# Low halves of all weight tiles made by VectorE, at the place in its order where GpSimd had them

## The reference

```python
h = _rmsnorm(x, norm_g[i])
u = h @ (w_in_a, w_in_b, w_in_c)[kind][j]          # mixer columns, 4 memory-query heads, gate
br = mixer_A | mixer_B | mixer_C                   # layers 0..3: A, B, C, A
mo = _mem_attend(mq, mem_k[i], mem_v[i])           # 4 heads over 256 memory tokens
y = concat([br, mo]) * silu(gate)
x = x + y @ w_out[i]
```

## Time and profile before

| | |
|---|---|
| median of 3 runs | 3066.82 us (3064.26 to 3069.39) |
| profiled execution | 3064.44 us, of which the span from first to last instruction is 3062.7 us |
| granted TensorE clock, mean over the span | 0.950 of full speed |
| PE, PEld | 2791.3 us (91%), 2613.0 us (85%) |
| DVE, ACT, POOL | 1301.4 us (42%), 1312.9 us (43%), 693.6 us (23%) |
| instructions in the span | 46628 |

### The profile page before, as it was taken

One profiled execution on the slowest core, in us unless ns is written; L12 is line 12 of the kernel. 1 busy time (PEld: TensorE's weight loads), 2 busy tenths in 40 slices (PEclk: granted clock), 3 DMA queues, 4 the chain that ended last, 5 costly groups with the idle time before them and its releaser, 6 DMA issues.

```text
span 3062.7 us, 46628 instructions
## 1 busy us (share of the span) xinstructions
PE 2791.3 (91%) x18936; PEld 2613.0 (85%) x18936; DVE 1301.4 (42%) x3217; ACT 1312.9 (43%) x2822; POOL 693.6 (23%) x389
## 2 busy tenths in 40 slices
PE   6989999989989999989988578888899989999987
PEld 4979999979989999979988567777699979999887
DVE  4045555551235665651232244544433054555542
ACT  3244454442244555542332245555533244544431
POOL 0212122205121222205120222222233212221112
PEclk9989999999999999989998789999899989999998
DMA  3111111123111111123110000000042111111121
GB/s 137 50 39 49 50 63 45 48 113 106 51 45 50 60 61 59 60 106 110 56 42 32 22 12 10 9 10 7 15 169 72 56 35 51 57 48 55 41 76 66
DMA packets 58197, 171.59 MB, mean 56 GB/s; under 512 B 6720, under 2 KB 15040, under 8 KB 57472
## 3 DMA queue, kind: packets, MB, share of 16 engines
q1 hardware_dynamic: 57984, 168.62, 16.1%
HBM read 134.67 MB, written 33.92 MB: 55 GB/s over the span
## 4 chain that ended last, share of the span: by engine, by line
PE 79%; ACT 9%; DVE 8%; issue 3%; DMA 0%; POOL 0%; SPq 0%; DVEq 0%; ACTq 0%
PE acc L1611 37%; PE acc L1687 10%; PE acc L1574 9%; PE scores L1632 8%; PE turned L1646 6%; PE scores L1528 4%; ACT prob L1098 4%; DVE prob L1354 2%; PE turned L1528 2%; PE scores L1506 1%; DVE pt_split L1383 1%; ACT pt_split L1110 1%; DVE y_sb L1410 1%; ACT prob L1101 1%; ACT w_hi L1028 1%
## 5 line engine op out<-in xcount | busy, mean ns | idle before, releaser
L1611 PE MATMUL acc<-h_split,w_hi 128*128 128x352 f32 (+2 forms) x4860 | 892.5, 330 | 45.0 <-ACT raw L982 13.2
L1611 PEld LDWEIGHTS acc<-h_split,w_hi 128*128 128x128 f32 x4860 | 791.7, 191 | 71.3 <-ACT raw L982 16.6
L1437 POOL TENSOR_TENSOR w_lo<-w_raw,w_hi 128x1024 fp32r<-128x1024 f32 (+2 forms) x154 | 332.2, 2159 | 1830.1 <-ACT w_hi L1028 1830.1
L1354 DVE CUSTOM_DVE_ANT_0 prob<-scores,bias 128x256 f32<-128x256 f32 (+9 forms) x576 | 337.7, 633 | 499.8 <-PE scores L1632 496.3
L1383 DVE TENSOR_TENSOR pt_split<-turned,pt_split 128x512 fp32r<-128x512 f32 (+4 forms) x564 | 303.3, 552 | 552.0 <-ACT pt_split L1110 551.6
L1687 PE MATMUL acc<-pt_split,v_split 128*64 128x256 f32 (+6 forms) x3486 | 501.4, 280 | 23.5 <-ACT pt_split L1110 7.4
L1611 PE MATMUL acc<-h_split,w_lo 128*128 128x352 f32 (+2 forms) x2430 | 453.6, 324 | 0.0
L1098 ACT ACTIVATE prob<-prob,stat 128x256 f32<-128x256 f32 (+9 forms) x468 | 303.7, 650 | 329.3 <-DVE stat L1354 329.2
L1687 PEld LDWEIGHTS acc<-pt_split,v_split 128*64 128x64 f32 (+2 forms) x3486 | 404.0, 161 | 41.2 <-issue 15.4
L1611 PEld LDWEIGHTS acc<-h_split,w_lo 128*128 128x128 f32 x2430 | 401.2, 189 | 0.1
L1646 PE MATMUL turned<-ident,prob 128*128 128x128 f32 (+2 forms) x1866 | 290.1, 280 | 98.4 <-DVE prob L1370 52.0
(11 more groups left out here) (124 smaller groups left out, 2796.9 us busy)
## 6 DMA issues: line engine op xcount, KB each, us to landing
w_raw<-w SPq DMA_DIRECT2D x132, 512.0 KB, 3.7
x_scr<-y_sb SPq DMA_DIRECT2D x24, 528.0 KB, 5.6
y_sb<-x_scr SPq DMA_DIRECT2D x24, 528.0 KB, 7.9
y_sb<-x_in SPq DMA_DIRECT2D x16, 528.0 KB, 10.5
mw_raw<-w SPq DMA_DIRECT2D x16, 512.0 KB, 7.4
bias<-rel_in SPq DMA_DIRECT2D x24, 320.0 KB, 4.0
raw<-kcache SPq DMA_DIRECT2D x18, 256.0 KB, 4.0
v_cache<-vcache SPq DMA_DIRECT2D x18, 256.0 KB, 4.0
```

The costliest lines, as they stand in the source:

```text
L1354: dve.tensor_tensor_reduce(out=prob[0:tile.rows, at:at + tile.width], in0=s_ps[lane][0:tile.rows, tile.at:tile.at + tile.width], in1=bias[ ...
L1437: pool.tensor_tensor(w_lo[:, n % 2, 0:wide], w_raw[:, n % 2, 0:wide], w_hi[:, n % 2, 0:wide].bitcast(F32), ALU.subtract).then_inc(wlo_made ...
L1611: ins = pe.matmul(acc[s.bank][:, 0:s.cols], w[ws][:, 128 * k:128 * k + 128], x(xs, k), start=k == 0 and y == 0, stop=k == s.k_tiles - 1 an ...
```

## The change

DVE makes `w_lo` of every tile, at the place of the `wsplit` in its own order; POOL no longer does. The arithmetic, the tiles, the semaphores and every other engine's order stay as they are. Of 156 tiles 154 change hands: 130 of 1024 columns, 12 of 384 and 12 of 256.

```diff
-            elif name == "wsplit" and item[1] < 2:
+            elif name == "wsplit":
                 n = item[1]
+                wide = 128 * plan.weights[n][2]
                 dve.wait_ge(*whi_made.upto(n))
-                dve.tensor_tensor(w_lo[:, n, :], w_raw[:, n, :], w_hi[:, n, :].bitcast(F32),
+                dve.tensor_tensor(w_lo[:, n % 2, 0:wide], w_raw[:, n % 2, 0:wide], w_hi[:, n % 2, 0:wide].bitcast(F32),
                                   ALU.subtract).then_inc(wlo_made.mark(n), 1)
...
-            if name == "wsplit" and item[1] >= 2:
-                n = item[1]
-                wide = 128 * plan.weights[n][2]
-                pool.wait_ge(*whi_made.upto(n))
-                pool.tensor_tensor(w_lo[:, n % 2, 0:wide], w_raw[:, n % 2, 0:wide],
-                                   w_hi[:, n % 2, 0:wide].bitcast(F32), ALU.subtract).then_inc(wlo_made.mark(n), 1)
-            elif name == "phase":
+            if name == "phase":
```

## The result

| | before | after |
|---|---|---|
| median | 3066.82 us (5 runs, 3063.80 to 3069.39) | 3080.22 us (5 runs, 3077.91 to 3085.82) |
| ratio, 95% interval | | 1.0053 [1.0039, 1.0066] |
| span of the profiled execution | 3062.7 us | 3076.1 us |
| granted clock of the profiled execution | 0.950 | 0.947 |

What follows compares the result with a forecast made beforehand. PE was taken as the bound, busy 91% of the span with 79% of the last chain. Terms 5.0 + 1.3 + 2.6 + 0.9 − 1.4 = +8.4 us on 3064.4 give 3072.8, forecast 3075 against the median, range 3064 to 3092.

Steps and rivals of the forecast that it cites:

- That nothing is gained by an earlier `w_lo`: No engine waited for POOL's tile and two buffers give slack, so having it 1.1 us earlier gains nothing.
- DVE isn't the bound: DVE gains about 168 us of work, from 1301 to about 1470 us, 48% of the span; not a bound.
- The places of A (+5.0): Ten decoded-unit starts in A: DVE 0.66 us late, PE's slack 0.24 at most; about 0.50 us lost each, +5.0.
- the starts (+1.3): First scores of each layer's memory jobs queue behind `w_lo`, so ACT's exponential starts 0.33 us late: 4 × 0.33 = +1.3.
- decoded units (+2.6) of the memory jobs: PE already waits 1.29 us for DVE's multiply; the new order puts it 0.66 us later: 4 × 0.66 = +2.6.
- Key parts (+0.9): First key part of the second memory job: exponentials move 0.66 us against 0.36 slack; 0.3 us in three layers, +0.9.
- B (−1.4): The norm's multiply no longer waits beside POOL's `w_lo`; PE regains 0.28 us in each of five jobs, −1.4.
- The output projections, costed at nothing in the sum: The 30 low halves standing in the output projections add no term to the sum; left to the rivals.
- The rival: Output projections: POOL's sum and `mw_lo` hold DVE's scalings; PE 1.12 us late per tile, +13.4, about 3088; chance 0.18.
- The clock, named as a rival on the faster side only: PE's mean granted clock rises from 0.950 to about 0.955, bringing back 14.5 us, about 3058; chance 0.08.
- the forecast's own range: Whole kernel: 3070.5 to 3080 us, with the small terms somewhat larger or smaller; chance 0.50.
- the band that it gave to contention: 3080 to 3094 us, if scalings in the output projections wait for POOL, once or twice in part; chance 0.18.

Runs made afterwards that it cites:

- Experiment 4: Changed kernel, but POOL keeps 33 low halves (21 at A's ten places and in memory jobs, 12 ahead of the scalings): 3065.43 us against 3065.13 before, ratio 1.0004.
- experiment 8: Changed kernel with output-projection scalings first and 24 low halves behind DVE's next scores: 3067.71 us against 3064.66 for the kernel before, ratio 1.0011.
- Experiment 5: Changed kernel, but DVE makes the low half twice in a row at the ten places of A: 3094.13 us, ratio 1.0099 to the kernel before.
- experiment 2: Changed kernel, but POOL makes the 30 low halves of the output projections: 3079.08 us, ratio 1.0047 to the kernel before.
- experiment 3: Changed kernel, but DVE does the output projections' two scalings ahead of the weight's low half: 3078.34 us, ratio 1.0050 to the kernel before.
- experiment 6: Changed kernel, but POOL's sum of squares in the four tiles adds 32 columns instead of 1056: 3076.97 us, ratio 1.0041 to the kernel before.
- experiment 7: Changed kernel, but POOL makes the memory weight's low half behind those of the two scaled slices: 3077.48 us, ratio 1.0042 to the kernel before.
- experiment 10: Kernel before, with only the ten low halves at the places of A moved to DVE: 3076.15 us, ratio 1.0037.
- experiment 1: Kernel before, with only the 30 low halves of the output projections moved to DVE: 3072.14 us against 3065.13, ratio 1.0027.
- experiment 9: Kernel before, with only the 14 low halves in the memory jobs moved to DVE: 3077.40 us against 3063.21, ratio 1.0046.
- experiment 11: Kernel before, with only the 16 low halves in B's mixer jobs moved to DVE: 3067.02 us against 3063.21, ratio 1.0007.
- experiment 12: Kernel before, with only the 62 low halves of the gate stages and C moved to DVE: 3067.70 us against 3063.21, ratio 1.0009.

## Why the prediction was right, and where not

- **That nothing is gained by an earlier `w_lo`, and that DVE isn't the bound:** right. Experiment 4 carries 121 of the moved instructions at no measurable cost, experiment 8 all 154 at 3 us.
- **The places of A (+5.0), the starts (+1.3) and decoded units (+2.6) of the memory jobs:** right in mechanism and size, 5.0, 1.5 and 2.7 in the trace. One name was wrong: the low half that arrives late at the places of A isn't the decoded unit's; it is the fourth unit's second chunk, which stands on DVE behind the decoded unit's scales. Experiment 5 shows that DVE's queue sets these ends, and experiment 8 that the order ahead of the low half is what costs. Read in the same way against the kernel before, the traces of experiments 2, 3, 5, 6, 7 and 10 have 5.0 to 5.1 at this step of the ten places, and those of 1, 4, 8, 9, 11 and 12, where no weight's low half stands ahead of it, 0.0 to 0.1.
- **Key parts (+0.9):** mis-sized, 0.2 where it could be read.
- **B (−1.4):** the mechanism is right, the multiply fell from 1214 to 634 ns; in the trace it is 0.50 us at each of five places, 2.5. Experiment 11 could not show it in the measured time; with the clock taken out (the table below, an estimate) it is −1.9.
- **The output projections, costed at nothing in the sum:** this is the step that failed. The rival held 0.18 of the chance, and it happened at each of the twelve places. Its schedule was right (sum, first scaling, `mw_lo`, second scaling, add), its price twice too high: 1.12 us each, where the trace shows 0.46 to 0.65. The first scaling took some 0.3 us between the two POOL operations, not 0.44, and the sum started 0.2 us before DVE's `w_lo` ended. That two operations are needed was right: with either of them out of the way (experiments 6 and 7) or the scalings first (3), PE's waits are gone, and only the traces that have the hand-over (the changed kernel's, 1 and 5) show the 7 us. "GPSIMD Engine Reference", § 8 Key points, of the Trainium skill says that the two engines contend where VectorE's instruction has two SBUF inputs; the 5.24 us for 0.87 us of work agree with it.
- **The clock, named as a rival on the faster side only:** incomplete, and priced too high. A straight line through each kernel's own runs (161 in all) gives 1.4 us more for each 0.001 of clock less; the prediction had 14.5 us for 0.005, twice that. At this rate, an estimate, the table takes the clock out of the mean times; clock and time stand against the kernel before on the same chip, the changed kernel's against all its 60 runs.

| kernel | waits (us) | clock lower by | mean time over (us) | at equal clock (us) |
|---|---|---|---|---|
| experiment 1 | 6.8 | 0.0017 | 7.9 | 5.6 |
| experiments 2, 3, 6, 7 | 7 | 0.0035 to 0.0039 | 12.6 to 14.8 | 7.6 to 9.5 |
| experiment 9 | 4.6 | 0.0064 | 14.7 | 5.9 |
| experiment 10 | 5.0 | 0.0022 | 11.9 | 8.9 |
| experiment 11 | −2.5 | 0.0028 | 2.0 | −1.9 |
| the change | 13.7 | 0.0040 | 17.4 | 12.0 |

Most of what the experiments cost beyond their waits goes with a lower clock; some 4 us of experiment 10 don't. Experiments 1 and 2, which share out the change between them, come to 14 at equal clock against its 12. Why the clock is lower isn't shown, and added waits alone aren't it: experiment 11 has none. Of the 15 stretches behind decoded units (two of them in the earlier trace rows) at which the prediction hoped for full speed, 6 had the low level before; in the changed kernel's trace 9 have it, and 10 in that of experiment 9, which leaves these units as they were.
- **The forecast of 3075:** 5 us low, at the very edge of the forecast's own range and in the band that it gave to contention. The waits of the output projections that the sum left out (+6.8) and B's larger gain (−1.1) account for that to within the spread of the runs. That the sum so mended meets the median to a microsecond is luck: the runs of one kernel spread over 5 to 18 us.

## What to carry to other kernels

Moving an instruction to an idle engine isn't free because the engine is idle: it is queued, in order, and what stands behind it must have the slack, so put it behind the work that others wait for (experiment 8 against the change: 3 us over the kernel before instead of 13). Look too at what the engine that gets free will do with its time: here POOL's next two operations moved up by 1.4 us against PE's work and into DVE's way. And set the granted clock beside every time: here kernels that differ by a few us of waits differ by up to 0.006 in mean clock, some 9 us by the estimate above, so a time that misses its sum of waits need not hide another wait.

## What the runs showed of the hardware

- Between two POOL operations that run back to back, one waiting DVE operation was served: the first scaling got through after the sum of squares (ACT reads its result at 705.09, 0.32 us after the sum's end), the second had to wait for all of `mw_lo`, which took 2.58 us instead of 2.42.
- Narrow subtractions on DVE aren't in proportion to their width: 1225 ns for 1024 columns, 554 for 384 and 425 for 256, not the 460 and 310 that the prediction took.
- TensorE's granted clock differs between executions over the same work: A's first stage took 417.9 us at 0.98 and 422.6 at 0.96, C's stream 395.0 at 0.93 and 398.4 at 0.92, each time in the kernel before and in experiment 9, which changes nothing there.
